# Moving the matmul operands of a two-block kernel off a common 2048-byte grid in SBUF

## The chip, the cores and the metric

The kernel runs on one core of one Trainium2 chip. The metric is the device time of one execution in microseconds; the lower, the better. The time before is 1351.55 us, the median of three runs (1351.45 to 1351.58).

## The reference

Two transformer blocks run one after the other over one sequence of 512 tokens of width 1024, in float32:

```python
def first_block(x, ...):
    h = h + hybrid_mixer(rms_norm(h, norm1_g), w_in, ...)   # gated conv + retention, @ w_out
    h = h + sq_relu_mlp(rms_norm(h, norm2_g), w_up, w_down) # relu(u @ w_up)**2 @ w_down
    return rms_norm(h, final_norm_g)

def second_block(x, c, ...):
    h = rmsnorm(x, g_norm1) * (1.0 + scale1) + shift1       # adaLN: c @ w_ada + b_ada
    ...                                                     # proj = h @ w_in
    merged = (sigmoid(gate_fox) * (y_fox @ w_branch_fox)    # forgetting attention, 8 heads
              + sigmoid(gate_dsa) * (y_dsa @ w_branch_dsa)) # top-k sparse attention, 8 heads
    x = x + gate1 * (merged @ w_out)
    x = x + gate2 * (square(relu(h2 @ w_mlp1)) @ w_mlp2)
    return rmsnorm(x, g_final)
```

The inner width of both MLPs is 4096. Nearly all the arithmetic is the product of a 512-token activation with a weight matrix of 1024 or 4096 rows.

## The kernel before

Activations are kept transposed: the partition is the feature within a chunk of 128, and along the partition come 8 chunks (KC) of 512 tokens (T). A chunk of one tensor is therefore 512 float32 values, 2048 bytes of each partition, and a tensor of eight chunks has 16,384 bytes of each partition.

A float32 product is made of three matmuls in the format float32r. Each operand is split into a high part (its float32r rounding) and a low part (what the rounding left), and high times high, high times low and low times high are added in PSUM. The tensors that hold such parts are:

- `w_hi` and `w_lo`: the parts of the weights, in four slots (SLOTS) of 1024 values each. A slot holds eight stationary blocks of 128 columns (512 bytes each) for most stages, and two moving blocks of 512 columns for each of two chunks in others.
- `u_hi` and `u_lo`: the parts of a norm's output (the norms' activations).
- `y_hi` and `y_lo`: the parts of the mixers' outputs, and of the MLPs' inner activation.
- `m_hi` and `m_lo`: the parts of the second block's merged activation. `q_up`, `q_dn` and `k_both` are the parts of queries and keys in its attention.

The work on a slot of weights goes through four engines in turn. SyncE starts the load of 512 KB into `raw` (line 343, helper `load`). ScalarE rounds it to `w_hi` (line 1213, helper `cast`). GpSimd subtracts and writes `w_lo` (line 542, helper `lo`). TensorE uses the slot for 24 matmuls of 512 columns and gives it back. The semaphores `raw_ready`, `hi_ready`, `lo_ready` and `used` carry this; the four slots let the engines before TensorE run ahead of it.

The main helper on TensorE is `unit` (line 566). The weights are stationary and the activation moves:

```python
for w, r in ((w_hi, r_hi), (w_hi, r_lo), (w_lo, r_hi)):
    last = pe.matmul(ps[0:cols, bank, :], w[:, s, c], r[:, k, :], ...)   # line 581
```

In the second block's value projections (`value_slot`, line 1008) and in its MLP's second half (`down_rows`, line 1127, and `last_down_rows`, line 1157) the roles are turned: 128 tokens of `u` or `y` are stationary and 512 columns of the weights move. `branch` (line 1071) and `two_units_early` (lines 921 to 925) are as `unit`. Every matmul of the program has a weight load of its own (LDWEIGHTS in the profile, engine PEld), which reads the next matmul's stationary operand while the present matmul streams its moving one.

The rest are short matmuls in plain float32: transposes against an identity matrix (`small`, lines 639, 974, 1096), the retention's inner products (lines 674 to 697, on the tensors `qf`, `kf`, `sdec`, `vtok`, `state`) and sums over partitions.

Tensors in SBUF are placed one behind the other in the order of their declaration; an ExitStack that is closed gives its room to what is declared next. One pad, `to_line`, of 72 values stands just before `xres`. With it `xres` starts at byte 32768 of the partition, and since all the large tensors behind it have sizes that are multiples of 2048, each of `u_hi`, `u_lo`, `y_hi`, `y_lo`, `raw`, `w_hi`, `w_lo`, `m_hi`, `m_lo`, `q_up`, `q_dn`, `k_both`, `vtoks` and `xg` starts at a multiple of 2048. The tensors declared ahead of the pad, and those of the first block behind the table `fades`, do not: modulo 512, `nt`, `nsq`, `nrs`, `small`, `ones` and `prob_evens` lie at 128, and `xtok`, `vtok`, `qf`, `kf`, `sdec`, `ktok`, `state`, `osb` and `acc` at 64.

Of the kernel before, what the change touches and what calls it, by code (L numbers as in the profile page):

```python
# [25 lines left out]
F32R = mybir.dt.float32r  # L26
# [4 lines left out]
P = 128  # L31
T = 512
NT = T // P
D = 1024
KC = D // P
# [9 lines left out]
SLOTS = 4  # L45
# [126 lines left out]
def build(nc, tab, x, norm1_g, w_in, conv_w, conv_norm_g, ret_norm_g, w_out, norm2_g, w_up, w_down,  # L172
# [30 lines left out]
    with ctx:  # L203
        def sb(name, shape, dt=F32, where=ctx):
            return where.enter_context(nc.sbuf_tensor(name, shape, dt))
# [31 lines left out]
        sb("to_line", [P, 72])  # L237

        xres = sb("xres", [P, KC, T])
        u_hi, u_lo = sb("u_hi", [P, KC, T], F32R), sb("u_lo", [P, KC, T], F32R)  # L240
        y_hi = sb("y_hi", [P, KC, T], F32R)
        scores = ExitStack()
        sb("y_lo_front", [P, NQ, T], where=scores)
        work = sb("work", [P, NT - 1, T], where=scores)
# [1 line left out]
        scores.close()  # L246
        y_lo = sb("y_lo", [P, KC, T], F32R)
        raw = sb("raw", [P, SLOTS, KC * P])
        w_hi, w_lo = sb("w_hi", [P, SLOTS, KC * P], F32R), sb("w_lo", [P, SLOTS, KC * P], F32R)

        one = ExitStack()
        fades = sb("fades", [P, P + 4 * NQ], where=one)
# [30 lines left out]
        two = ExitStack()  # L283
        merge = ExitStack()
        vtoks = sb("vtoks", [P, 2, NT, QW], where=merge)
        q_up, q_dn = sb("q_up", [P, 4, T], F32R, where=merge), sb("q_dn", [P, 4, T], F32R, where=merge)
        merge.close()
        m_hi, m_lo = sb("m_hi", [P, KC, T], F32R, where=two), sb("m_lo", [P, KC, T], F32R, where=two)
        keys_done = ExitStack()
        gates = sb("gates", [P, 4, T], where=keys_done)  # L290
        keys_done.close()
# [2169 lines left out]
```

## Time and profile before

| | |
|---|---|
| median of three runs | 1351.55 us |
| the profiled execution, its own time | 1352.54 us |
| its span, first to last instruction | 1350.7 us |
| TensorE matmuls busy | 1339.7 us (99%) |
| TensorE weight loads busy | 1094.2 us (81%) |
| VectorE / ScalarE / GpSimd busy | 56% / 39% / 42% |
| mean granted TensorE clock | 0.998 |
| DMA moved | 155.7 MB, mean 115 GB/s |

The time of an execution holds 1.84 us that lie outside the span. A matmul's row gives the time from its start to its modelled end, and matmuls overlap: rows of 389 ns start 227 ns apart. The distance between starts is what counts for the time, and the rows of the chain give it, as the length of a run of matmuls over their number. Weight loads stand in rows of their own.

### The profile page before, as it was taken

To read this page: it belongs to the slowest core of one execution; us is meant where nothing else is said; L and a number is where in the kernel's file an instruction comes from. 1 tells how busy PE (TensorE), PEld (TensorE's weight loads), DVE (VectorE), ACT (ScalarE), POOL (GpSimd) and SP (SyncE) were. 2 spreads that over 40 slices of the span, in tenths; PEclk is the share of its full clock that TensorE was granted. 3 is DMA by queue.
4 is the path that set the end of the run, shared out by engine and by line. 5 is a ranking of instruction groups with operands and counts; after the bars stand their busy time and mean duration, and the time that the engine had idled before them with its cause. 6 is when DMAs were issued, how large, how long until landed. Compare 5 with 4: busy or idle time off the path is not lost.

```text
span 1350.7 us, 18066 instructions
## 1 busy us (share of the span) xinstructions
PE 1339.7 (99%) x6376; PEld 1094.2 (81%) x6380; DVE 756.1 (56%) x1085; ACT 525.9 (39%) x830; POOL 563.0 (42%) x230
## 2 busy tenths in 40 slices
PE   9999999999999999999999999999999999999998
PEld 8888878888888888886877777888878888888887
DVE  4555578475664655877788774434563241432355
ACT  6344234422323224254366665232355133142333
POOL 5334344454553635524222223444434534345351
PEclk9999999999999999999999999999999999999999
DMA  7232245555655645423212323333423423324221
GB/s 230 80 97 78 91 130 171 164 167 177 198 168 163 183 143 166 112 91 95 63 56 86 95 63 94 109 94 105 129 73 100 125 78 109 93 79 123 78 94 63
DMA packets 212807, 155.74 MB, mean 115 GB/s; under 512 B 8932, under 2 KB 193760, under 8 KB 212744
## 3 DMA queue, kind: packets, MB, share of 16 engines
q1 hardware_dynamic: 212280, 154.43, 38.4%
q8 instruction: 39, 0.64, 0.2%
q10 hardware_dynamic: 464, 0.48, 0.1%
q14 instruction: 24, 0.20, 0.0%
HBM read 152.75 MB, written 4.74 MB: 117 GB/s over the span
## 4 chain that ended last, share of the span: by engine, by line
PE 53%; DVE 1%; ACT 1%; issue 0%; POOL 0%; ACTq 0%; DVEq 0%
PE ps L581 28%; PE ps L1127 11%; PE ps L1071 3%; PE ps L1008 3%; PE ps L987 1%; PE ps L974 1%; PE ps L1157 1%; PE ps L960 1%; PE ps L961 1%; PE ps L947 0%; PE ps L964 0%; PE ps L921 0%; PE ps L925 0%; PE ps L922 0%; PE ps L1096 0%
## 5 line engine op out<-in xcount | busy, mean ns | idle before, releaser
L542 POOL TENSOR_TENSOR w_lo<-raw,w_hi 128x1024 fp32r<-128x1024 f32 x222 | 560.0, 2530 | 758.1 <-ACT w_hi L1213 738.0
L581 PE MATMUL ps<-u_hi,w_hi 128*128 128x512 f32 x944 | 378.5, 401 | 0.8 <-POOL w_lo L542 0.5
L581 PE MATMUL ps<-u_hi,w_lo 128*128 128x512 f32 x944 | 368.3, 390 | 0.0
L581 PE MATMUL ps<-u_lo,w_hi 128*128 128x512 f32 x944 | 367.5, 389 | 0.0
L1213 ACT ACTIVATE w_hi<-raw 128x1024 fp32r<-128x1024 f32 x222 | 231.6, 1053 | 289.3 <-PE ps L581 116.8
L581 PEld LDWEIGHTS ps<-u_hi,w_lo 128*128 128x128 f32 x944 | 177.2, 188 | 37.7
L581 PEld LDWEIGHTS ps<-u_hi,w_hi 128*128 128x128 f32 x944 | 178.1, 189 | 36.3 <-issue 1.6
L581 PEld LDWEIGHTS ps<-u_lo,w_hi 128*128 128x128 f32 x944 | 177.6, 188 | 34.9 <-issue 1.0
L581 PE MATMUL ps<-y_hi,w_hi 128*128 128x512 f32 x320 | 125.3, 391 | 0.1
L581 PE MATMUL ps<-y_hi,w_lo 128*128 128x512 f32 x320 | 124.5, 389 | 0.0
L581 PE MATMUL ps<-y_lo,w_hi 128*128 128x512 f32 x320 | 124.5, 389 | 0.0
L1432 ACT ACTIVATE nsq<-ps 128x512 f32<-128x512 f32 x64 | 38.3, 598 | 198.6 <-PE ps L581 193.6
L1127 PE MATMUL ps<-w_hi,y_hi 128*128 128x512 f32 x224 | 87.1, 389 | 0.0
L1127 PE MATMUL ps<-w_lo,y_hi 128*128 128x512 f32 x224 | 87.1, 389 | 0.0
L1127 PE MATMUL ps<-w_hi,y_lo 128*128 128x512 f32 x224 | 87.1, 389 | 0.0
L2000 DVE SCALAR_TENSOR_TENSOR acc<-adaw,vec,acc 128x1536 f32<-128x1536 f32 x28 | 82.5, 2946 | 1.9 <-DVE y_lo L2054 1.5
L2110 DVE TENSOR_TENSOR nt<-nsq 128x512 f32<-128x512 f32 x32 | 27.9, 873 | 98.1 <-ACT nsq L1432 98.0
L2049 DVE TENSOR_TENSOR nt<-nsq 128x512 f32<-128x512 f32 x32 | 24.3, 758 | 84.5 <-ACT nsq L1432 83.9
L581 PEld LDWEIGHTS ps<-y_hi,w_hi 128*128 128x128 f32 x320 | 60.1, 188 | 13.9 <-issue 1.1
L581 PEld LDWEIGHTS ps<-y_lo,w_hi 128*128 128x128 f32 x320 | 60.1, 188 | 12.5 <-issue 0.2
L581 PEld LDWEIGHTS ps<-y_hi,w_lo 128*128 128x128 f32 x320 | 60.1, 188 | 12.6
L2132 DVE SCALAR_TENSOR_TENSOR nt<-ps,rinv,gate_row 128x512 f32<-128x512 f32 x21 | 15.8, 751 | 92.4 <-PE ps L1127 92.4
(317 smaller groups left out, 1878.8 us busy)
## 6 DMA issues: line engine op xcount, KB each, us to landing
raw<-w_in SPq DMA_DIRECT2D x69, 512.0 KB, 3.7
raw<-w_mlp SPq DMA_DIRECT2D x64, 512.0 KB, 3.8
adaw<-w_ada SPq DMA_DIRECT2D x32, 768.0 KB, 4.6
raw<-w_up SPq DMA_DIRECT2D x32, 512.0 KB, 6.1
raw<-w_down SPq DMA_DIRECT2D x32, 512.0 KB, 5.5
raw<-w_out SPq DMA_DIRECT2D x16, 512.0 KB, 4.2
bias_rows<-bias_rows SPq DMA_DIRECT2D x4, 635.0 KB
xtok<-x SPq DMA_DIRECT2D x4, 512.0 KB, 7.3
```

The costliest lines, as they stand in the source:

```text
L542: pool.tensor_tensor(w_lo[:, s, :], raw[:, s, :], w_hi[:, s, :], ALU.subtract).then_inc(lo_ready[s], 1)
L581: last = pe.matmul(ps[0:cols, bank, :], w[:, s, c], r[:, k, :], start=(k == ks[0] and w is w_hi and r is r_hi), stop=(k == ks[-1] and w is ...
L960: pe.matmul(ps[:, bank, 0:keys], q_up[:, at, q], k_both[:, at, 0:keys], start=True, stop=False)
L1008: last = pe.matmul(ps[:, i, :], u[:, k, t], w[:, s, c], start=(k == 0 and u is u_hi and w is w_hi), stop=(k == KC - 1 and u is u_lo))
L1071: last = pe.matmul(ps[:, b, :], w[:, 2, c], r[:, k, :], start=(k == k0 and w is w_hi and r is y_hi), stop=(k == k0 + NQ - 1 and w is w_lo))
L1127: last = pe.matmul(ps[:, i, :], h[:, k, t], w[:, s, c], start=(k == 0 and h is y_hi and w is w_hi), stop=(k == KC - 1 and h is y_lo))
L1213: act.activation(w_hi[:, s, :], raw[:, s, :], ACT.Copy).then_inc(hi_ready[s], 1)
L1432: act.activation(nsq[:, s % 2, :], ps[:, s, :], ACT.Relu).then_inc(bank_free[s], 1)
L2000: dve.scalar_tensor_tensor(a, adaw[:, b, :], c, a, ALU.mult, ALU.add).then_inc(sem("acc_done"), 1)
L2049: dve.tensor_tensor(nt[:, s % 2, :], nsq[:, s % 2, :], nsq[:, s % 2, :], ALU.mult).then_inc(sem("mlp_sq"), 1)
L2110: dve.tensor_tensor(nt[:, s % 2, :], nsq[:, s % 2, :], nsq[:, s % 2, :], ALU.mult).then_inc(sem("mlp_sq"), 1)
L2132: dve.scalar_tensor_tensor(gated[i], ps[:, i, :], facts[:, i:i + 1], gate_row[:, c], ALU.mult, ALU.mult).then_inc(bank_free[i], 1)
```

## The change

Pads are added between tensors. A pad is a tensor that nothing reads or writes. No instruction is added, removed or put elsewhere on any engine, and no semaphore is changed; the operands' addresses are all that differs.

```diff
         xres = sb("xres", [P, KC, T])
-        u_hi, u_lo = sb("u_hi", [P, KC, T], F32R), sb("u_lo", [P, KC, T], F32R)
+        sb("to_line1", [P, 64])
+        u_hi = sb("u_hi", [P, KC, T], F32R)
+        sb("to_line2", [P, 32])
+        u_lo = sb("u_lo", [P, KC, T], F32R)
+        sb("to_line3", [P, 48])
         y_hi = sb("y_hi", [P, KC, T], F32R)
+        sb("to_line4", [P, 96])
         scores = ExitStack()
         sb("y_lo_front", [P, NQ, T], where=scores)
         work = sb("work", [P, NT - 1, T], where=scores)
...
         y_lo = sb("y_lo", [P, KC, T], F32R)
         raw = sb("raw", [P, SLOTS, KC * P])
-        w_hi, w_lo = sb("w_hi", [P, SLOTS, KC * P], F32R), sb("w_lo", [P, SLOTS, KC * P], F32R)
+        sb("to_line5", [P, 16])
+        w_hi = sb("w_hi", [P, SLOTS, KC * P], F32R)
+        w_lo = sb("w_lo", [P, SLOTS, KC * P], F32R)
+        sb("to_line7", [P, 48])
...
         vtoks = sb("vtoks", [P, 2, NT, QW], where=merge)
+        sb("to_line_q", [P, 32], where=merge)
         q_up, q_dn = sb("q_up", [P, 4, T], F32R, where=merge), sb("q_dn", [P, 4, T], F32R, where=merge)
         merge.close()
-        m_hi, m_lo = sb("m_hi", [P, KC, T], F32R, where=two), sb("m_lo", [P, KC, T], F32R, where=two)
+        m_hi = sb("m_hi", [P, KC, T], F32R, where=two)
+        sb("to_line_m", [P, 32], where=two)
+        m_lo = sb("m_lo", [P, KC, T], F32R, where=two)
```

A pad of n values moves all that follows by 4n bytes. Adding them up gives the start of each tensor modulo 512:

| tensor | before | after |
|---|---|---|
| `w_hi`, `w_lo` | 0 | 0 |
| `u_hi` | 0 | 256 |
| `u_lo` | 0 | 384 |
| `y_hi` | 0 | 64 |
| `y_lo`, `work`, `rfin`, `raw` | 0 | 448 |
| `m_hi`, `vtoks` | 0 | 192 |
| `m_lo`, `q_up`, `q_dn`, `k_both`, `gates`, `xg`, `tab2`, `sel` | 0 | 320 |
| `xtok`, `vtok`, `qf`, `kf`, `sdec`, `acc` and others of the first block | 64 | 256 |
| `xres` and all that is declared ahead of it | as before | as before |

Every start is a multiple of 64 bytes, before and after.

## Rows read from the trace of the kernel before

**Rows 1.** The page: busy time by engine, and TensorE's granted clock in 40 slices
```profile
span 1350.7 us, 18066 instructions
PE 1339.7 (99%) x6376; PEld 1094.2 (81%) x6380; DVE 756.1 (56%) x1085; ACT 525.9 (39%) x830; POOL 563.0 (42%) x230
...
PEclk9999999999999999999999999999999999999999
```

**Rows 2.** The chain of waits in time: start us, length us, instructions and their number
```profile
849.10 5.44 PE ps L1071 x24
...
947.02 43.53 PE ps L581 x192
...
1040.33 43.52 PE ps L1127 x192
```

**Rows 3.** Matmul groups by shape: count, then busy us, mean ns, idle before
```profile
L581 PE MATMUL ps<-u_hi,w_hi 128*128 128x512 f32 x944 | 378.5, 401 | 0.8 <-POOL w_lo L542 0.5 <-issue 0.2
...
L581 PE MATMUL ps<-y_hi,w_hi 128*128 128x512 f32 x320 | 125.3, 391 | 0.1
...
L1127 PE MATMUL ps<-w_hi,y_hi 128*128 128x512 f32 x224 | 87.1, 389 | 0.0
...
L1008 PE MATMUL ps<-w_hi,u_hi 128*128 128x512 f32 x64 | 26.4, 413 | 0.0
...
L1071 PE MATMUL ps<-y_hi,w_hi 128*128 128x512 f32 x64 | 24.9, 389 | 0.0
...
L581 PE MATMUL ps<-m_hi,w_hi 128*128 128x512 f32 x64 | 24.9, 389 | 0.0
...
L727 PE MATMUL ps<-w_hi,u_hi 128*128 128x512 f32 x32 | 12.3, 400 | 0.5 <-issue 0.5
...
L1157 PE MATMUL ps<-w_hi,y_hi 128*128 128x512 f32 x28 | 10.9, 389 | 0.0
...
L1096 PE MATMUL ps<-small,xres 128*128 128x128 f32 x32 | 4.0, 272 | 0.0
```

**Rows 4.** Timeline of matmuls around 56 us: start us, us, instruction
```profile
55.88 0.39 PE L581 MATMUL ps<-u_lo,w_hi 128*128 128x512 f32 x1
56.11 0.39 PE L581 MATMUL ps<-u_hi,w_lo 128*128 128x512 f32 x1
56.34 0.60 PE L695 MATMUL ps<-vtok,sdec 128*128 x4
```

**Rows 5.** Weight load groups by shape: count, then busy us, mean ns
```profile
L1127 PEld LDWEIGHTS ps<-w_hi,y_hi 128*128 128x128 f32 x224 | 42.0, 188 | 8.8
...
L974 PEld LDWEIGHTS ps<-small,prob_evens 128*128 128x128 f32 x64 | 7.8, 140 | 3.9 <-issue 1.4 <-DVE prob_odds L2335 1.2
...
L695 PEld LDWEIGHTS ps<-vtok,sdec 128*128 128x128 f32 x32 | 4.8, 191 | 0.3
...
L1096 PEld LDWEIGHTS ps<-small,xres 128*128 128x128 f32 x32 | 3.7, 140 | 1.2 <-issue 1.1
```

**Rows 6.** Timeline of matmuls around 1006 us: four transposes
```profile
1006.57 0.60 PE L1096 MATMUL ps<-small,xres 128*128 128x128 f32 x4
```

**Rows 7.** ScalarE and GpSimd groups by shape, same columns
```profile
L1213 ACT ACTIVATE w_hi<-raw 128x1024 fp32r<-128x1024 f32 x222 | 231.6, 1053 | 289.3 <-PE ps L581 116.8 <-PE ps L1127 104.1 <-PE ps L1071 24.8
...
L1434 ACT ACTIVATE y_hi<-nsq 128x512 f32 x56 | 35.4, 633 | 7.5
...
L1264 ACT ACTIVATE u_hi<-xg 128x512 fp32r<-128x512 f32 x8 | 5.1, 633 | 2.8 <-DVE xg L1802 2.3
...
L542 POOL TENSOR_TENSOR w_lo<-raw,w_hi 128x1024 fp32r<-128x1024 f32 x222 | 560.0, 2530 | 758.1 <-ACT w_hi L1213 738.0 <-DVE u_lo L1786 20.1
```

**Rows 8.** Waits: who waited for whom, us in total, times, longest
```profile
POOL w_lo L542 <- ACT w_hi L1213: 738.0, 181, 16.2
...
ACT w_hi L1213 <- DMA raw<-w_up: 15.6, 6, 10.7
```

**Rows 9.** DMA issues: count, KB each, median us from issue to landing
```profile
raw<-w_up SPq DMA_DIRECT2D x32, 512.0 KB, 6.1
```

## The prediction

> **What bounds the kernel now.** I read the page first: TensorE's matmuls are busy for 1339.7 of 1350.7 us, no other compute engine is above 56%, and the granted clock is 9 tenths or more in every slice, so it stands at its upper level, 2.4 GHz [rows 1]. The clock is not what is lost. Next the chain of waits, which shows what the busy time is made of. A run of 192 matmuls with weights stationary takes 43.53 us, one with the activation stationary 43.52 us, and 24 matmuls of the branches 5.44 us [rows 2]. Each comes to the same distance between two starts: 43.53 / 192 = 226.7 ns. At 2.4 GHz 512 columns need 512 / 2.4 = 213.3 ns. So each matmul pays 226.7 - 213.3 = 13.4 ns beyond its columns, in every stage and in either role. In all these stages the moving and the stationary operand start at a multiple of 512 bytes, so these runs can't tell whether the 13.4 ns come from that.
>
> Then the groups by shape, for the number of matmuls the change can touch. Of each group three kinds stand in the profile (high-high, high-low, low-high), equally many: 3 x (944 + 320 + 224 + 64 + 64 + 64 + 32 + 28) = 3 x 1740 = 5220 matmuls of 512 columns [rows 3]. At 226.7 ns they are 1183 us, 88% of the span. One nanosecond on each of them is 5.2 us, or 0.39% of the time. No other effect of an address comes near that weight, so the whole question is what one matmul's distance does.
>
> **The change part by part.** It adds no instruction, DMA or wait and takes none away; the order on all engines is unchanged. So there is nothing to add but durations, and each part of the cost is an answer to "does this engine's time depend on the offset".
>
> *TensorE, distance between matmuls: 0 taken.* While a matmul streams, the next one's 512 bytes per partition of weights are read. The only way in which the new offsets could pay is that both reads now meet in some part of SBUF and no longer would. Before the change such meetings at another offset already occur, where a float32r matmul is followed by a short float32 one. At 56.11 us a matmul on `u_hi` (moving, offset 0) streams while the weights of line 695 are read, from `sdec`, at offset 64; the next start is at 56.34, 0.23 us later, as after its neighbour (55.88 to 56.11, also 0.23) [rows 4]. There are four such places, one for each of the four heads. Had the offset of 64 removed the whole 13.4 ns, 0.21 would stand there. The rows are in hundredths and the follower is another kind of matmul, so this speaks against a gain without excluding one of a few ns. The transposes say the same on the side of weight loads: on `xres`, at offset 0, and on `prob_evens`, at offset 128, both against `small` at 128 as the moving side, a load takes 140 ns in the mean either way [rows 5]. Four transposes on `xres` span 0.60 us with a mean of 272 ns for one, so their starts are (600 - 272) / 3 = 109 ns apart [rows 3, 6], and that is how long the read of 512 bytes of weights may last at the most.
>
> There is a second reason, from the same numbers. In 109 ns the moving side passes 109 / 226.7 x 2048 = 985 bytes while the weights pass 512. One stream overtakes the other by 473 bytes, nearly a whole period of 512. Wherever they start, they come past each other about once in each matmul. If a meeting costs something, another offset shifts its moment within the matmul and hardly removes it.
>
> Bounds for this term: downwards, all 13.4 ns on 5220 matmuls, -70 us. Upwards, the nearest rows are weight loads: those at an offset of 64 take 191 ns (line 695) where the aligned ones take 188 (line 1127) [rows 5]; these 3 ns also hold the step from float32r to float32. If all of them reached the matmul's distance, that is 3 x 5220 = +15.7 us. I take 0, since the row nearest to the case, the mixed pair at 56.11, reads 0.
>
> The Trainium skill has two rules that bear on this. "SBUF — State Buffer", section "Door 1: The DMA port swizzle", says that SBUF is read in lines of 16 bytes and that crossing into a new line costs. By it nothing changes, because every new start is a multiple of 64 and a stream touches as many lines as before; no row here shows a line. "TensorE: Matmul & The Clock Gate", section "Wait — 56ns, not 53.3ns?", gives back-to-back matmuls N / 2.4 + about 2.5 ns, 215.8 for 512 columns. The trace disagrees with that by 11 ns (226.7), and this is the best argument that something avoidable is in the gap; an estimate by that page is 11 x 5220 = -57 us, were the gap closed. Its section "Step-by-step: what each phase is for" gives TensorE two independent read ports, by which a weight load takes nothing from a running matmul, wherever it lies.
>
> *ScalarE and VectorE: 0.* ScalarE takes 633 ns from `nsq` (at 128) to `y_hi` (at 0), and 633 ns from `xg` to `u_hi`, both at 0 [rows 7]. Relative offsets of 0 and 128 cost the same. These engines wait for TensorE and not the other way round.
>
> *GpSimd: 0 on the path.* Its subtraction reads `raw` and `w_hi`, both at 0 before, at 448 and 0 after, and takes 2530 ns [rows 7]. A unit of 24 matmuls lasts 5.44 us [rows 2], so it could take twice as long before TensorE waited for it in the steady state. It spends 738.0 us waiting for ScalarE's rounding [rows 8], and the matmuls on `u_hi` waited for it 0.5 us in all [rows 3]. If that cover were gone in the few places where a stage begins, a tenth more on one subtraction is 0.25 us each, below 2 us for all.
>
> *DMA into `raw`: 0 on the path.* The blocks of 512 bytes now land at an offset of 448 and no longer fill one grid cell. The slowest large group lands 6.1 us after its issue [rows 9]. A slot comes round every 4 x 5.44 = 21.8 us, of which the load, the rounding of 1.05 and the subtraction of 2.53 fill 9.7. ScalarE waited for a DMA of `w_up` six times, 15.6 us [rows 8], and those waits are shorter than the lead. A load slower by 10% adds 0.6 us where it shows at all, which is in the first microseconds. I take 0, and 1 us as its upper end.
>
> The sum is 0 against the profiled execution's 1352.5 us (span 1350.7 and 1.8 around it). That one execution lies 1.0 us above the median of the runs, and with a change of 0 the median stays: 1351.5 us.
>
> **The rivals.**
>
> *Faster, the collision is real.* The 13.4 ns are a clash of the two reads when both start at the same place modulo 512. For it: the gap is the same in all stages, and all stages are aligned alike. Against it: the pair at 56.11, the passing of the two streams, and that no row names such a clash anywhere. Wholly removed it gives 1351.5 - 70 = 1282 us. More likely is a part, because the six activation tensors get six different offsets and some would help and others not: between 1 and 5 ns in the mean, 5 to 26 us, so 1325 to 1346 us, with 1340 as its middle.
>
> *Slower, a stream that starts off the grid needs one access more.* A moving operand of 2048 bytes touches five cells of 512 bytes instead of four, and a stationary one of 512 bytes two instead of one, in `down_rows` and `value_slot`. Its place is the matmul's distance, its price the 3 ns between the two loads above: 1351.5 + 15.7 = 1367 us. It decides against my forecast from 0.5 ns per matmul on (2.6 us). For it: the 191 against 188. Against it: that `xres` and `prob_evens` have the same 140 ns.
>
> *The change doesn't do what it says.* The relative offset that counts could be finer than 64 bytes, or be one against banks of another size. Then all offsets stay equal in effect, and the time is the forecast's.
>
> **How the numbers follow.** No effect on the distance (with the last rival in it): 0.63. Collision removed, in part 0.11 and wholly 0.08: 0.19. Slower per matmul: 0.18. A change within 0.2%, 2.7 us, is about what a measurement of this kernel can't tell from none; of the first case 0.01 is given to the fast side, for small gains elsewhere, and the rest lies within it, which gives 0.19 + 0.01 = 0.20 faster, 0.62 same, 0.18 slower. The likeliest case alone has 1349 to 1354. The range must take in the small effects of either sign: down to 1338 it holds half of the partial gain, up to 1363 the slower case up to 2.2 ns per matmul. Left out are the whole gain, the rest of the partial one, and the slower case from there on, together about 0.2.
>
> **What would show it.** In the chain after, the runs of 192 matmuls say all: 43.5 us means no effect, 41.0 the whole gap closed, 44.1 the slower case. If the two roles part (line 581 with `u` at 256 and 384, line 1127 with `y` at 64 and 448, `m` at 192 and 320), the offsets matter singly. GpSimd's 2530 ns and the loads' 6.1 us should stay within a few per cent. I would be wrong if the distance of any of these runs moved by 0.5 ns or more, or if matmuls began to wait for `w_lo`.

## The result: 1374.3 us, 1.7% slower

The changed kernel takes 1374.26 us (median of three runs, 1373.69 to 1374.80) against 1351.55 before: a ratio of 1.0168, with a 95% interval of 1.0145 to 1.0191. The prediction was 1351.5 us, with a range up to 1363; the time lies outside it, 22.7 us above the forecast.

The page of the changed kernel shows where not to look. The busy times of the other engines stand within 1 us of what they were (VectorE 755.3 for 756.1, GpSimd 562.9 for 563.0), and only TensorE's own grew, from 1339.7 us [rows 1]:

```profile
span 1373.0 us, 18066 instructions
PE 1362.6 (99%) x6376; PEld 1094.8 (80%) x6380; DVE 755.3 (55%) x1085; ACT 525.8 (38%) x830; POOL 562.9 (41%) x230
...
PEclk9999999999999999999999999999999999999999
```

The chain of the changed kernel (start us, length us, instructions and their number) gives the distance between matmuls, stage by stage. It answers to [rows 2]; the pads moved the line numbers by 11 (581 is 592, 1127 is 1138, 1071 is 1082):

```profile
849.04 5.53 PE ps L1082 x24
...
865.60 11.19 PE ps L592 x48
...
882.31 10.99 PE ps L592 x48
...
959.83 44.37 PE ps L592 x192
...
1054.91 44.52 PE ps L1138 x192
1099.43 44.78 PE ps L592 x192
```

The branches go from 226.7 to 230.4 ns per matmul (5.53 / 24), the output projection on `m` to 231.1, the down stage with `y` stationary to 231.9, and the stage on `u` of the second MLP to 233.2 (44.78 / 192). Every stage slows, each by another amount: these four by 3.7 to 6.5 ns. Spread over the 5220 matmuls of the prediction, 22.7 us are 4.3 ns each. The two rows of 48 matmuls are worth a second look: they are the same code on the same operands (`u` over `w`), and one takes 0.20 us more than the other, 233.1 against 229.0 ns per matmul.

What the prediction held to be harmless was so. GpSimd's subtraction keeps its mean, and the loads of `w_up` land in 6.6 us instead of 6.1 [rows 7, 9], which nothing waits for: the matmuls on `u_hi` still waited 0.5 us in all for `w_lo` [rows 3].

```profile
L553 POOL TENSOR_TENSOR w_lo<-raw,w_hi 128x1024 fp32r<-128x1024 f32 x222 | 559.9, 2530 | 779.5 <-ACT w_hi L1224 759.0
L592 PE MATMUL ps<-u_hi,w_hi 128*128 128x512 f32 x944 | 384.1, 407 | 0.5 <-POOL w_lo L553 0.5
...
raw<-w_up SPq DMA_DIRECT2D x32, 512.0 KB, 6.6
```

### The profile page after: what moved, and what is told of

Its sections match the earlier page's. It is cut to its first block, busy times and chain, and to the rows that moved or that the text cites. A ratio compares the mean times of both kernels' runs of the same rounds, so it can differ in the third digit from the quotient of the medians.

```text
span 1373.0 us, 18066 instructions
## 1 busy us (share of the span) xinstructions
PE 1362.6 (99%) x6376; PEld 1094.8 (80%) x6380; DVE 755.3 (55%) x1085; ACT 525.8 (38%) x830; POOL 562.9 (41%) x230
## 4 chain that ended last, share of the span: by engine, by line
PE 53%; DVE 1%; ACT 1%; issue 0%; POOL 0%; ACTq 0%; DVEq 0%
PE ps L592 28%; PE ps L1138 11%; PE ps L1082 3%; PE ps L1019 2%; PE ps L1168 2%; PE ps L998 1%; PE ps L985 1%; PE ps L971 1%; PE ps L972 1%; PE ps L958 0%; PE ps L975 0%; PE ps L932 0%; PE ps L933 0%; PE ps L936 0%; DVE nt L2279 0%
## 5 line engine op out<-in xcount | busy, mean ns | idle before, releaser
L592 PE MATMUL ps<-u_hi,w_hi 128*128 128x512 f32 x944 | 384.1, 407 | 0.5 <-POOL w_lo L553 0.5
L592 PE MATMUL ps<-u_lo,w_hi 128*128 128x512 f32 x944 | 372.6, 395 | 0.0
```

## The experiments

**A grid of offsets, matmuls alone.** The kernel loads `x`, rounds it into two tensors `mov` and `sta` that both start on the 2048-byte grid, and runs groups such as this one, one source line for each pair of offsets:

```python
for j in range(36):
    last = pe.matmul(ps[:, j % 8, :], s(0, j % 8), m(64, j % 8), start=True, stop=True)
```

> A kernel of matmuls alone, which leaves the whole computation out: 33 groups of 36 float32r matmuls of 512 columns, each with its own weight load, with nothing beside them. One source line per group; the moving operand starts at an offset m and the stationary one at s from a 2048-byte grid: first m = 0, s = 0, then m = 4, 16, 32, 64, 128, 192, 256, 320, 384, 448, 512, 1024 with s = 0; again 0, 0; then the same twelve s with m = 0; 0, 0; then both at 16, 64, 192, 256 and 448; 0, 0. Theory A (an operand's own start off a 512-byte grid costs a matmul time): 226.7 ns between starts at 0, 512 and 1024, 229 to 236 at every other m, and both equal is as slow as one alone. Theory B (only the difference of the two starts counts): 226.7 for both equal. Theory C (the matmuls slow down in the kernel because of work or DMA beside them, which the offsets of raw changed): 226.7 in all 33 groups.

The timeline of its matmuls (start us, length us, instructions; the distance is the difference of two rows' starts over 36):

```profile
35.93 8.32 PE L70 MATMUL ps<-mov,sta 128*128 128x512 f32 x36
44.09 8.67 PE L72 MATMUL ps<-mov,sta 128*128 128x512 f32 x36
...
69.33 8.41 PE L78 MATMUL ps<-mov,sta 128*128 128x512 f32 x36
77.58 8.53 PE L80 MATMUL ps<-mov,sta 128*128 128x512 f32 x36
85.95 8.56 PE L82 MATMUL ps<-mov,sta 128*128 128x512 f32 x36
94.35 8.34 PE L84 MATMUL ps<-mov,sta 128*128 128x512 f32 x36
...
177.25 8.56 PE L104 MATMUL ps<-mov,sta 128*128 128x512 f32 x36
185.64 8.53 PE L106 MATMUL ps<-mov,sta 128*128 128x512 f32 x36
194.01 8.41 PE L108 MATMUL ps<-mov,sta 128*128 128x512 f32 x36
202.26 8.34 PE L110 MATMUL ps<-mov,sta 128*128 128x512 f32 x36
...
268.24 8.33 PE L126 MATMUL ps<-mov,sta 128*128 128x512 f32 x36
276.40 8.33 PE L128 MATMUL ps<-mov,sta 128*128 128x512 f32 x36
```

Lines 70 to 84 have the moving operand at 0, 4, ..., 64, 128, 192 and 256 over a stationary one at 0. Lines 104 to 110 have the stationary one at 64, 128, 192 and 256 under a moving one at 0. Line 126 has both at 64. So (44.09 - 35.93) / 36 = 226.7 ns for 0 over 0, and in the same way for the rest. Each value holds the turn-over, the first few matmuls of a group, in which the distance still changes from that of the group before; where the text says "once settled", the mean of the last 18 distances of a group is meant, by the starts in the trace.

```
offset in bytes            64     128    192    256    320    384    448
moving off, stationary 0   229.2  232.5  233.3  227.2  229.2  232.5  233.6
stationary off, moving 0   233.1  232.5  229.2  227.2  233.3  232.2  229.2
both off (64, 192, 448)    226.7         226.7                       227.2
```

Three things stand in this table, for offsets that are multiples of 64. The values repeat after 256 bytes. The second row is the first one mirrored: moving at 64 costs what stationary at 192 costs, so it is the moving start minus the stationary start, modulo 256, that counts. And with no difference between them both may lie off the grid (at 64, 192, 256 and 448) at no cost. At finer offsets the rule does not hold: moving alone at 4, 16 and 32, it is 236.4, 231.4 and 233.3 ns, with both at 16 still 230.3, and with stationary alone at 16 it is 233.3, where the second grid below has 226.9 for the same difference (moving at 240). Theory C, work beside the matmuls, falls: nothing runs beside them here. No pair of the 33 groups is below 226.7.

**Everything at 64.** In the whole kernel the first pad becomes 64 bytes longer, so that all large tensors shift together:

```diff
-        sb("to_line", [P, 72])
+        sb("to_line", [P, 88])
```

> The kernel before with the first pad 64 bytes longer (88 values for 72), so that xres, u, y, raw, w, m, q, k all start at 64 modulo 512, with no difference between them. Theory A (own start off the grid costs): as slow as the change or near it, 1365 to 1380 us, runs of 192 matmuls at 44.3 us or more. Theory B (the difference of the two starts counts): 1351.5 us, within 1, and 43.5 us for 192.

It measured 1351.92 us against 1351.71 for the kernel before beside it (ratio 1.0001, 0.9992 to 1.0011), with 43.52 us for 192 matmuls in both roles. An operand's own start is not what costs; the difference is. That is Theory B.

**Only u off.**

```diff
+        sb("pad1", [P, 64])
+        u_hi = sb("u_hi", [P, KC, T], F32R)
+        sb("pad2", [P, 32])
+        u_lo = sb("u_lo", [P, KC, T], F32R)
+        sb("pad3", [P, 32])
```

> Only u_hi (256) and u_lo (384) off the grid; y, raw, w, m, q, k stay at 0 modulo 512. Theories A and B alike: the stages on u slow down as in the changed kernel (233.2 ns where it has 44.78 us for 192), which is 6.5 ns on some 2950 matmuls, 15 to 19 us: 1367 to 1371 us; the stages on y and m stay at 226.7. Theory C (raw's offset and the DMAs do it): 1351.5 us.

It measured 1361.25 us against 1351.71 (1.0068, 1.0051 to 1.0084): +9.5 us, half of what was expected. Its chain tells why:

```profile
953.90 43.53 PE ps L585 x192
...
1047.81 43.53 PE ps L1131 x192
1091.34 43.95 PE ps L585 x192
```

The stage on `u` takes 43.95 us, 228.9 ns per matmul, and not the 44.78 of the changed kernel, though `u` and `w` have the same offsets modulo 512 in both. The stages on `m` (953.90) and `y` (1047.81) are at their old 43.53.

**Only raw off.**

```diff
+        sb("pad1", [P, 112])
         raw = sb("raw", [P, SLOTS, KC * P])
+        sb("pad2", [P, 16])
```

> Only raw off the grid, at 448, where the loads land; all matmul operands at 0 modulo 512. Theories A and B: 1351.5 us, within 1, though the loads of w_up may take 6.6 us as in the changed kernel and not 6.1. Theory C: 1360 us or more.

1353.04 us against 1351.71 (1.0006, 0.9996 to 1.0016); the chain has 43.52 us for 192 matmuls, while the loads of `w_up` take 6.8 us. Where the loads land does not matter within what can be told.

**A second grid.**

> A kernel of matmuls alone again, which leaves the whole computation out. Theory D (what counts is the moving start minus the stationary start modulo 256; from the first grid: 226.7 ns at 0, 229.0 at 64, 232.4 at 128, 233.3 at 192): (a) triples as in unit with the changed kernel's offsets (moving 256, 384, 256, stationary 0) take 226.7 + 232.4 + 226.7 = 686 ns per triple, whatever ran before. Theory E (the state in which a group is entered also counts): the same triple takes 686 when entered from aligned matmuls and about 700, as in the changed kernel, when entered from short float32 ones or from a group at 192. (b) moving 0 and 256 in turn: 226.7; 0 and 128 in turn: 229.5; 0 and 64: 227.8. (c) the step between 0 and 64 and between 192 and 256 shows whether the curve is smooth. (d) both operands at 4 or 32: over 226.7 if a 64-byte grid also counts, both at 128: 226.7. (e) 128, 256 or 384 columns at 0, 64, 192: the surcharge is the same in ns if it belongs to the weight load. (f) bfloat16: near 216 to 220 at 0, 0 if the 13.4 ns belong to the 512 bytes of a float32 load, 226.7 if they belong to every load.

The distances in the timeline, all between starts:

```profile
42.61 5.60 PE L91 MATMUL ps<-mov,sta 128*128 128x512 f32 x24
48.05 11.15 PE L93 MATMUL ps<-mov,sta 128*128 128x512 f32 x48
59.04 2.84 PE L95 MATMUL ps<-otok,xtok 128*128 128x128 f32 x24
61.63 11.34 PE L97 MATMUL ps<-mov,sta 128*128 128x512 f32 x48
72.81 5.61 PE L99 MATMUL ps<-mov,sta 128*128 128x512 f32 x24
...
350.79 4.52 PE L173 MATMUL ps<-mov,sta 128*128 128x256 f32 x36
355.15 4.40 PE L175 MATMUL ps<-mov,sta 128*128 128x256 f32 x36
359.40 4.40 PE L177 MATMUL ps<-mov,sta 128*128 128x256 f32 x36
...
387.89 7.94 PE L187 MATMUL ps<-movb,stab 128*128 128x512 bf16 x36
395.67 7.93 PE L189 MATMUL ps<-movb,stab 128*128 128x512 bf16 x36
...
426.75 20.76 PE L197 MATMUL ps<-otok,xtok 128*128 128x512 f32 x48
447.35 20.76 PE L199 MATMUL ps<-otok,xtok 128*128 128x512 f32 x48
```

Lines 93 and 97 are the same triple, the change's 256, 384, 256 over 0. Entered from aligned matmuls (line 93) 48 of them take 10.99 us, 229.0 ns each; entered from short plain float32 ones (line 97) 11.18 us, 232.9 with the turn-over, and 231.1 once settled. Theory D alone falls: the same operands have more than one lasting pace. Theory E's size was wrong, as it had about 233 for this entry and for the one from a group at 192, which settles at 231.1 as well.

Moving at 64 over 192 and at 192 over 64 both take 232.5 ns, and at 320 over 64 it settles at 226.7: the difference modulo 256 also rules where both operands are off. Theory D's sums for moving starts in turn missed one of three: 0 and 256 gave the 226.7 expected, 0 and 128 gave 230.0 for 229.5, but 0 and 64 gave 231.4 for 227.8, more than either start alone (226.7 and 229.2). So a mixture is not the mean of its parts. Between the multiples of 64 the curve isn't smooth: moving at 80 or 112 takes 231, at 208 234.7, and at 240 226.9.

In bfloat16 (lines 187 and 189, moving at 0 and 64) the distance is 7.78 / 36 = 216.1 ns and 216 at the other offsets tried, and in plain float32 it is 429 ns whatever the offset (lines 197 and 199, 20.60 / 48). With 256 columns (lines 173 to 177, offsets 0, 64, 192) the offsets even help: once settled, 117.8 against 120.0 ns. With 128 columns nothing changes. Both operands at 32 or at 128 settle at 226.7; both at 4 at 239. So the loss belongs to float32r matmuls of 384 columns or more (384 at 192 took 1.4 ns more than at 0 once settled, 512 up to 7).

**All activations at 256.** Pads of 64 values before `u_hi`, after `y_lo`, and around `m_hi` and `m_lo`:

```diff
+        sb("pad1", [P, 64])
         u_hi = sb("u_hi", [P, KC, T], F32R)
...
         y_lo = sb("y_lo", [P, KC, T], F32R)
+        sb("pad5", [P, 64])
```

> u, y and m all at 256 modulo 512, the weights' parts, raw, q and k at 0. Theory D (period of 256): 1351.5 us, within 1, 43.5 us for 192 matmuls in both roles. If the period were 512, or any distance from the weights cost: 1360 to 1385 us.

1351.47 us against 1351.83 (0.9994, 0.9985 to 1.0004), and 43.52 us for 192 matmuls in both roles. The period of 256 holds in the kernel.

**Only y and m off**, at the change's offsets, by the same kind of pads.

> y_hi at 64, y_lo at 448, m_hi at 192, m_lo at 320, as in the change; u, raw, w, q, k at 0. Theory D: the stages on y and m as in the changed kernel (230.6 to 231.9 ns), about 4.6 ns on 2100 matmuls, +9.6 us: 1361; the stages on u at 226.7. With the 9.5 us of u alone that makes 19, and the change cost 22.7, so Theory E (history) has to account for the remaining 3 to 4 us by a slower pattern on u in the changed kernel.

1361.20 us against 1351.83 (1.0066, 1.0049 to 1.0082): +9.4 us, as expected. Its chain:

```profile
949.98 44.37 PE ps L589 x192
...
1044.14 44.51 PE ps L1135 x192
1088.65 43.54 PE ps L589 x192
```

The stages on `m` and `y` have the changed kernel's lengths to 0.01 us, and the aligned stage on `u` runs at 43.54 although it comes right behind a stage that is off: an aligned pair falls back to 226.7 whatever ran before. Together with +9.5 for `u` alone this makes 18.9 of the 22.7 us.

**All activations at 192.** As the kernel with 256, with pads of 48 and 80.

> u, y and m all at 192 modulo 512, everything else at 0: one common distance from the weights. Theory D: activations moving, 192 - 0 = 192, +6.6 ns on 4248 matmuls; activations stationary, 0 - 192 = 64 modulo 256, +2.3 ns on 1044: +30.4 us, 1382 us, with 44.8 us for 192 matmuls on u and 44.0 in the down stage. Theory F (the cost comes from a change of offset between consecutive matmuls, not from a distance that stays): 1351.5 us.

1378.90 us against 1351.83 (1.0192, 1.0175 to 1.0209). Theory F falls, since a common offset costs as well. The chain:

```profile
1060.75 43.96 PE ps L1133 x192
1104.71 44.80 PE ps L587 x192
1149.51 44.80 PE ps L1133 x192
```

The stage on `u` takes 44.80, 233.3 ns, as the grid says for moving at 192. The down stage takes 43.96 (229.0, the grid's value for stationary at 192) in one round and 44.80 in the next, with the same code and operands: two paces again. Even with the slower pace in it the kernel is 3 us below the estimate of 1382, since the stages with short matmuls or waits between their long ones grew by less than the grid's values.

**A third grid**, on the width of the stationary operand and on the memory.

> Matmuls alone, which leaves the whole computation out. First part: the stationary operand has 128, 96, 64 or 32 columns (512, 384, 256, 128 bytes), each at moving offsets 0, 64, 128 and 192. Theory G (the 13.4 ns at offset 0 and the surcharge at other offsets are both time that the weight load's read takes from the moving stream): 13.4 ns shrinks in proportion, 226.7, 223.3, 220.0, 216.7 ns, and the surcharge of 2 to 7 ns shrinks with it. Theory H (both belong to the matmul, whatever is loaded): 226.7 and 229 to 233 at every width. Second part: one and the same group (the change's triple 256, 384, 256 over 0; or moving 0 over 192) entered from nine, then seven different groups. Theory E (more than one lasting pattern for the same operands): the triple settles at 686.7, 693 or about 700 ns by what came before, the single pair at 229 or 233.3. Without such memory: one value each after at most six matmuls.

The second part, in the timeline:

```profile
197.79 8.40 PE L131 MATMUL ps<-mov,sta 128*128 128x512 f32 x36
206.03 5.60 PE L133 MATMUL ps<-mov,sta 128*128 128x512 f32 x24
...
230.83 5.70 PE L141 MATMUL ps<-mov,sta 128*128 128x512 f32 x24
236.37 8.55 PE L143 MATMUL ps<-mov,sta 128*128 128x512 f32 x36
244.75 5.62 PE L145 MATMUL ps<-mov,sta 128*128 128x512 f32 x24
250.21 5.67 PE L147 MATMUL ps<-mov,sta 128*128 128x512 f32 x24
```

Line 131 is the triple 256, 384, 256 entered from aligned matmuls, line 143 the same entered from 64, 448, 64, which are the offsets of `y`. They take 8.24 / 36 = 228.9 and (244.75 - 236.37) / 36 = 232.8 ns, 233.3 once settled. Those are the two paces of the stage on `u` in the whole kernel: 228.9 where the stage before it, on `y`, is aligned (only u off), and 233.2 where `y` is off too (the change). The triple settles at 233.3 also from moving 64, from stationary 64, from 384 columns and from 128 columns of float32r, and at 231.1 from moving 192, from bfloat16 and from plain float32. The pair with the stationary operand at 192 settles at 229.0 from six entries and at 233.3 from one, moving 192, as in the kernel with all activations at 192. The groups at 0 over 0 between them are at 226.7 every time (line 145: 5.46 / 24 = 227.5 with the turn-over).

The first part refutes both G and H. At offset 0, stationary operands of 96, 64 and 32 columns take 230, 230 and 232 ns once settled, more than the 226.7 of 128 columns, and at 32 columns the four offsets no longer differ (231 to 232). The 13.4 ns are not a share of the load's bytes; the dependence on the offset does go away with the shortest load. In between it turns: with 96 columns the cheapest of the four offsets is 192, with 64 columns it is 64 (228.3 ns). Of the widths tried, equal starts are the best case for 128 stationary columns only. Lines 101 and 107 are the 96 columns at 0 and at 192, (90.00 - 81.69) / 36 = 230.8 and (114.96 - 106.72) / 36 = 228.9 ns:

```profile
81.69 8.46 PE L101 MATMUL ps<-mov,sta 128*96 128x512 f32 x36
90.00 8.55 PE L103 MATMUL ps<-mov,sta 128*96 128x512 f32 x36
...
106.72 8.40 PE L107 MATMUL ps<-mov,sta 128*96 128x512 f32 x36
114.96 8.44 PE L109 MATMUL ps<-mov,sta 128*64 128x512 f32 x36
```

**All activations at 64.** The mirror of 192, with pads of 16 and 112.

> u, y and m all at 64 modulo 512, everything else at 0: the mirror of the run with 192. By the first grid, activations moving lie 64 ahead: +2.3 ns on 4248 matmuls; activations stationary, 0 - 64 = 192 modulo 256: +6.6 ns on 1044. Sum +9.8 + 6.9 = +16.7 us, 1368 us; if some stages settle in the slower pattern, as the down stages did at 192, up to 1382. Whether it is below the 1378.9 of the run with 192 tells whether the sign of the distance counts.

1366.55 us against 1352.41 beside it (1.0108, 1.0091 to 1.0125): near the 1368, and 12 us below the kernel at 192. The direction of the distance counts, as the mirrored rows of the first grid have it. That the sum came out so near is in part luck, for the stages on `u` in the second MLP show two paces too, where the sum of 1368 had the faster one for all:

```profile
1092.58 44.80 PE ps L587 x192
...
1182.18 43.96 PE ps L587 x192
```

## Why the prediction was wrong

**What bounds the kernel** was read rightly: one nanosecond on each of 5220 matmuls is 5.2 us, and nothing but the distance between matmuls moved. The 5220 leave out 72 matmuls of lines 897 to 925 that use `u` as well; with these 5292 the share is the same to 0.1 ns.

**The step that failed** is the term "TensorE, distance between matmuls: 0 taken". It was mis-sized: the runs show +4.3 ns per matmul (22.7 us over 5220), beyond the 3 ns at which its upper bound stood, because the distance depends on the moving start minus the stationary start. The term rested on three readings.

- The pair at 56.11 us [rows 4] read 0.23 us with a difference of 64 and was taken for the row nearest to the case. Its figure can't show the effect: starts in hundredths of a microsecond read 0.23 at 226.7 ns and at 233.3 ns alike. And its weight load belongs to a plain float32 matmul. The second grid shows plain float32 pairs to be deaf to offsets (429 ns at 0, 64 and 192); the mixed pair was not tried, but a row with one float32 operand is no evidence on float32r pairs. That nothing else in the trace had a float32r matmul off the grid was the fact to weigh: the trace of before could not show this operation, and the range should have gone by that.
- The transposes [rows 5, 6] are plain float32 with 128 columns, for which the second grid has 111.7 ns at 0 and at 192, once settled. And what was compared was the length of weight loads, which doesn't move in float32r either.
- The argument that two streams which pass each other once meet at any offset left out that the time may depend on how they are placed against each other. The grid shows that it does, and that a difference of zero is the cheap case.

**The bounds.** The upper one, +15.7 us, came from 191 against 188 ns of weight loads [rows 5]. The first grid shows float32r loads at 187 to 189 ns at every offset, and the second has plain float32 loads at 190 to 192 with equal starts. So these 3 ns were the step from float32r to float32, and the surcharge lies between the matmuls, not in the load's row. The lower one, -70 us, was the gap closed; no pair of operands came below 226.7 ns with 512 columns.

**The rivals.** "Slower, a stream that starts off the grid" had the sign, at 0.18, and the wrong mechanism: with everything at 64, each operand starts off the grid and nothing is lost. "Faster, the collision is real" had an interaction of the two reads in it, which the runs bear out, but with the sign turned: equal starts are the best case. "The change doesn't do what it says" had the period right in part, as `u_hi` at 256 counts as equal to 0, but the other offsets are not equal in effect. The Trainium skill's rule of lines of 16 bytes ("SBUF — State Buffer", "Door 1: The DMA port swizzle") would have had no change, as every start is a multiple of 64; the grid disagrees, by 2.5 to 6.6 ns at 64, 128 and 192. The Trainium skill's two independent read ports ("TensorE: Matmul & The Clock Gate", "Step-by-step: what each phase is for") would have the load's place not matter; the mirrored rows disagree. The Trainium skill's N / 2.4 + about 2.5 ns ("TensorE: Matmul & The Clock Gate", "Wait — 56ns, not 53.3ns?"), 215.8 for 512 columns, agrees with bfloat16 here (216.1); the further 11 ns came with float32r in every run here, and no offset tried took them away.

**GpSimd, ScalarE, VectorE, DMA** at 0: right, and shown for `raw` by a run of its own.

Where the 22.7 us went: 9.5 is the offset of `u` as such and 9.4 that of `y` and `m`, each by a run alone. The remaining 3.8 is put down to the slower pace of the `u` stages behind `y` stages that are off. In the second MLP this is 3 x (44.78 - 43.95) = 2.5 us, read from the chains. In the first MLP it is as much: its first stage of 192 matmuls on `u` lasts 367.45 - 322.66 = 44.79 us in the changed kernel, and 43.95 with only `u` off. These are its first row in the timeline and the first of the stage behind it:

```profile
322.66 0.39 PE L592 MATMUL ps<-u_hi,w_hi 128*128 128x512 f32 x1
...
367.45 0.40 PE L592 MATMUL ps<-y_hi,w_hi 128*128 128x512 f32 x1
```

Summed from start to start over the traces, the stages on `u` grew by 14.2 us in the changed kernel and by 8.1 with only `u` off, so the slower pace is worth 6 us there. The 3.8 is a difference of medians whose intervals are 2 to 3 us wide to each side, and can't be told from 6. The short matmuls, on tensors that the change moved as well (`q_up`, `vtoks`, those of the first block), took 0.1 us more in all, waits included, so no loss shows there.

What stays open is the mechanism. The runs show the law at multiples of 64 (the difference modulo 256, float32r, long streams, a load of 128 columns) and the memory, but not the part of the chip that makes it, nor why a narrower stationary operand is slower at offset 0. What ran before isn't the whole of the memory either: the rows of 48 matmuls on `u` in the changed kernel all follow a branch on `y`, and take 11.19 and 10.99 us in turn. A meeting of the two reads in some bank is in keeping with most of it and is not shown.

## What to carry to other kernels

Place the moving and the stationary operands of float32r matmuls (512 columns moving, 128 stationary) so that their starts are equal modulo 256 bytes; then the grid itself didn't matter down to 32 bytes. A padding tensor that shifts some operands against the others costs up to 3% of each matmul, and no placement that was tried beat the kernel before. With other widths the best offset can be another one. And where the trace holds no instance of an operation in the new form, a neighbour in another format is no evidence of zero: measure a grid of it first.

## What the runs showed of the hardware

- The distance between float32r matmuls of 512 columns is 226.7 ns at equal starts modulo 256, 229.2 at moving minus stationary = 64, 232.5 at 128, 233.3 at 192, with starts at multiples of 64 and a stationary operand of 128 columns.
- bfloat16 takes 216 ns and plain float32 429 ns at every offset tried.
- The same operands can settle at different paces (228.9, 231.1 or 233.3 ns; 229.0 or 233.3 ns), by what ran before, and stay there for at least a whole stage of 192 matmuls. Equal starts bring it back to 226.7.
- With 256 moving columns equal starts are the slower case, 120.0 against 117.8 ns once settled.
- Below multiples of 64 the difference is not enough: both operands at 16 take 230, both at 4 take 239 ns, and moving at 240 over 0 takes 226.9 where moving at 0 over 16 takes 233.3.
